# A decoder layer on eight cores: RMS norms as an epilogue on the products, layer norm sums beside the convolution, and the orders at both ends

## What is computed

```python
x = x + 0.5 * swiglu_ffn(rms_norm(x, ffn1_norm), ffn1_w_gu, ffn1_w_down)
# token_mixer on h = rms_norm(x, mix_norm); p = h @ w_in, split in 6 parts of 2048
u = gelu(ua);  v = layer_norm(gelu(va), ln_v_g, ln_v_b)
y_a = chunk_spatial_gating(u, v, w_s, b_s) @ w_pa     # causal, chunks of 128 tokens
g = glu_a * sigmoid(glu_b)
c = conv_31_taps_depthwise(g) + b_dw
c = silu(layer_norm(c, ln_c_g, ln_c_b));  y_b = c @ w_pb
x = x + (sigmoid(gate_a) * y_a + sigmoid(gate_b) * y_b) @ w_out
x = x + 0.5 * swiglu_ffn(rms_norm(x, ffn2_norm), ffn2_w_gu, ffn2_w_down)
y = rms_norm(x, final_norm)
```

## Time and profile before

| | |
|---|---|
| median of three runs | 3339.24 us |
| the profiled execution | 3340.61 us, span 3339.1 us on core 4 |
| spans of the eight cores | 3331.6 to 3339.1 us |
| TensorE (PE) busy | 3232.5 us, 97% of the span, 21555 matmuls |
| VectorE (DVE) busy | 856.8 us, 26%, 1448 instructions |
| ScalarE (ACT) busy | 467.0 us, 14%, 909 instructions |
| GpSimd (POOL) busy | 128.6 us, 4%, almost only DMA issues |
| mean granted TensorE clock, core 4 | 0.985 of 2.4 GHz |
| DMA | 284.30 MB moved, mean 85 GB/s |

### The profile page before, as it was taken

One profiled execution on the slowest core, in us unless ns is written; L12 is line 12 of the kernel. 1 busy time (PEld: TensorE's weight loads), 2 busy tenths in 40 slices (PEclk: granted clock), 3 DMA queues, 4 the chain that ended last, 5 costly groups with the idle time before them and its releaser, 6 DMA issues.

```text
span 3339.1 us, 51314 instructions; the slowest of 8 cores (3331.6 to 3339.1 us)
## 1 busy us (share of the span) xinstructions
PE 3232.5 (97%) x21555; PEld 2059.6 (62%) x21556; DVE 856.8 (26%) x1448; ACT 467.0 (14%) x909; POOL 128.6 (4%) x246
## 2 busy tenths in 40 slices
PE   5999999999999999898999999999999999999997
PEld 2566666666665576677666666666666666666664
DVE  2212113112114443326531111114212112112115
ACT  3100000000002121147210101002100000000002
POOL 0000000000000000000000000000000000000000
PEclk8999999999999999999999999999999999999998
DMA  6425624424427555522423333373334434334434
GB/s 162 73 54 104 108 54 81 75 54 88 76 54 174 110 120 118 118 59 51 106 53 76 76 76 68 64 187 68 64 60 86 76 57 84 69 63 84 76 53 125
DMA packets 74112, 284.30 MB, mean 85 GB/s; under 512 B 9888, under 2 KB 36768, under 8 KB 52000
## 3 DMA queue, kind: packets, MB, share of 16 engines
q0 software_dynamic: 34848, 216.62, 36.6%
q1 hardware_dynamic: 39040, 64.40, 6.8%
HBM read 468.14 MB, written 32.87 MB: 150 GB/s over the span
## 4 chain that ended last, share of the span: by engine, by line
PE 94%; DVE 2%; ACT 1%; DMA 1%; issue 1%; SPq 0%; DVEq 0%; ACTq 0%
PE ps L192 94%; ACT arena L195 1%; DVE arena L205 1%; DMA arena<-xin 1%; DVE arena L198 1%; ACT L195 0%; DVE arena L209 0%; DMA vsamp<-arena 0%; DMA arena<-gd 0%; DMA gd<-arena 0%; SPq L976 0%; DVEq L967 0%; DVE arena L201 0%; DVEq L953 0%; ACTq L967 0%
## 5 line engine op out<-in xcount | busy, mean ns | idle before, releaser
L192 PE MATMUL ps<-arena 128*128 128x364 bf16 (+5 forms) x21555 | 3232.5, 312 | 86.1 <-ACT arena L195 48.5
L192 PEld LDWEIGHTS ps<-arena 128*128 128x128 bf16 (+1 forms) x21556 | 2059.6, 98 | 1258.6 <-issue 129.7
L198 DVE TENSOR_TENSOR arena<-arena,ps 128x364 bf16<-128x364 f32 (+9 forms) x472 | 236.9, 514 | 1681.4 <-PE ps L192 1668.7
L195 ACT ACTIVATE arena<-ps 128x364 f32<-128x364 f32 (+1 forms) x528 | 242.0, 464 | 2404.6 <-PE ps L192 2359.3
L205 DVE SCALAR_TENSOR_TENSOR arena<-ps,arena 128x364 f32<-128x364 f32 (+5 forms) x451 | 241.1, 539 | 500.2 <-PE ps L192 499.9
L198 DVE TENSOR_TENSOR arena<-arena 128x512 bf16<-128x512 f32 (+7 forms) x168 | 185.3, 1115 | 67.1 <-PE ps L192 44.9
L195 ACT ACTIVATE arena<-arena 128x364 bf16<-128x364 f32 (+6 forms) x276 | 152.8, 631 | 270.0 <-PE ps L192 194.2
L205 DVE SCALAR_TENSOR_TENSOR arena<-arena 128x364 bf16<-128x364 f32 (+4 forms) x196 | 101.2, 593 | 1.8 <-DVE arena L209 0.2
L976 POOL DMA_DIRECT2D arena<-w_gu x88 | 46.8, 532 | 1178.0 <-PE ps L192 1112.9
L976 POOL DMA_DIRECT2D arena<-w_dn x64 | 33.9, 530 | 772.5 <-PE ps L192 772.5
L195 ACT ACTIVATE arena<-ps,arena 128x272 bf16<-128x272 f32 (+3 forms) x76 | 38.0, 500 | 113.3 <-PE ps L192 113.2
(11 more groups left out here) (10 smaller groups left out, 15.9 us busy)
## 6 DMA issues: line engine op xcount, KB each, us to landing
arena<-w_gu POOLq DMA_DIRECT2D x88, 1024.0 KB, 8.9
arena<-w_dn POOLq DMA_DIRECT2D x64, 704.0 KB, 7.1
arena<-w_glu POOLq DMA_DIRECT2D x16, 1024.0 KB, 10.3
arena<-w_gate POOLq DMA_DIRECT2D x16, 1024.0 KB, 9.4
arena<-w_pab POOLq DMA_DIRECT2D x16, 1024.0 KB, 9.7
arena<-w_v POOLq DMA_DIRECT2D x8, 1024.0 KB, 9.3
arena<-w_u POOLq DMA_DIRECT2D x8, 1024.0 KB, 8.1
arena<-w_out POOLq DMA_DIRECT2D x8, 1024.0 KB, 9.9
```

Source lines behind the costliest of these rows:

```text
L192: return P.op("pe", lambda e: e.matmul(out, lhsT, rhs, start=start, stop=stop), deps)
L195: return P.op("act", lambda e: e.activation(out=out, in_=in_, func=func, **kw), deps)
L198: return P.op("dve", lambda e: e.tensor_tensor(out=out, in0=in0, in1=in1, op=op), deps)
```

## The change

**Segments and columns.** The segments are 384, 384, 350 (then 320). In each chunk of 128 tokens the columns are stored by phase (token 4q + j at 32j + q), masks, spatial weights and halo are permuted alike on the host, and the last V tile has 64 rows instead of 94.

**The norms.** H is now x * g alone, written by ACT as each row is finished; rstd multiplies the products afterwards. DVE does that, so DVE now lets go of the banks of gate, GLU's b, U and the gates. For V, rstd goes through DRAM into a scale by partition (`RV`) of ACT's gelu.

```diff
+            def gate_part(bank, lg, s):
+                x0, n = segs[s]
+                gi_, bg = bank
+                ti, tmp, tfree = TMPS.get()
+                e = tt(tmp[:, 0:n], bg[:, 0:n], RSTD[:, x0:x0 + n], ALU.mult, deps=[lg, rstd[s]] + tfree)
+                banks.release(gi_, [e])
+                return ti, tmp, act(tmp[:, 0:n], tmp[:, 0:n], AF.Silu, deps=[e])
+
+            def up_part(bank, lu, jj, s, gp):
+                x0, n = segs[s]
+                ui_, bu = bank
+                ti, tmp, ea = gp
+                e = tt(tmp[:, 0:n], tmp[:, 0:n], RSTD[:, x0:x0 + n], ALU.mult, deps=[ea])
+                ed = tt(HID[:, jj, x0:x0 + n], tmp[:, 0:n], bu[:, 0:n], ALU.mult, deps=[e, lu, hid_free[s]])
+                banks.release(ui_, [ed])
+                TMPS.release(ti, [ed])
+                hid[s] = ed
```

```diff
+            def row(self, k, dep):
+                self.flush()
+                x0, n = self.x0, self.n
+                X = self.Xs[self.s][:, k, 0:n]
+                si, sq, sfree = self.ring.get()
+                self.pend.append((k, si, sq[:, 0:n], act(sq[:, 0:n], X, AF.Square, deps=[dep] + sfree)))
+                if self.Hout is not None:
+                    self.out[(self.s, k)] = act(self.Hout[:, k, x0:x0 + n], X, AF.Identity, deps=self.hdep + [ev_pv],
+                                                scale=pvc(self.gidx, k))
...
+                n = self.n
+                for (k, si, sq, ea) in self.pend:
+                    if k < self.direct:
+                        if self.ev is None:
+                            self.ev = ts(self.acc, sq, 1.0, 0.0, ALU.mult, ALU.add, deps=[ea])
+                        else:
+                            self.ev = tt(self.acc, self.acc, sq, ALU.add, deps=[ea, self.ev])
...
-            return [step(k) for k in range(KC)] + [finish]
+                        if self.bank is None:
+                            bi, bk, bfree = stat_banks.get()
+                            self.bank = (bi, bk)
+                            for q, (pi_, pt, e) in enumerate(self.parts):
+                                lm = mm(bk[:, 0:n], ONES, pt[:, 0:n], q == 0, False, deps=[e, e_ones] + bfree)
+                                if pi_ is not None:
+                                    self.ring.release(pi_, [lm])
+                        self.lm = mm(self.bank[1][:, 0:n], ONES, sq, False, k == KC - 1, deps=[ea])
+                        self.ring.release(si, [self.lm])
```

```diff
+            def units_by_row(tiles, s, tok):
+                x0, n = segs[s]
+                got = [(banks.get(), banks.get()) for _ in tiles]
+                last = {}
+                for k in range(KC):
+                    tok.prep(k)
+                    for (jj, slot, lev), ((_g, bg, gfree), (_u, bu, ufree)) in zip(tiles, got):
+                        W = wk(slot)
+                        lg = mm(bg[:, 0:n], W[:, k, 0:128], Hv[:, k, x0:x0 + n], k == 0, k == KC - 1,
+                                deps=[lev, hready[(s, k)]] + (gfree if k == 0 else []))
+                        last[jj] = (lg, mm(bu[:, 0:n], W[:, k, 128:256], Hv[:, k, x0:x0 + n], k == 0, k == KC - 1,
+                                           deps=(ufree if k == 0 else [])))
+                    tok.sum(k)
+                tok.finish()
+                for (jj, slot, lev), ((gi_, bg, _f), (ui_, bu, _h)) in zip(tiles, got):
+                    up_part((ui_, bu), last[jj][1], jj, s, gate_part((gi_, bg), last[jj][0], s))
```

**The convolution's layer norm.** A square on ACT of each conv output, four additions of 544 elements on DVE (`ln_sum`) per channel group, 16 matmuls of 272 in all behind that (`ln_phase`), `ln_apply` in phase order, and one contiguous silu of 1088 for each row. Five V tiles stand ahead of conv(15):

```diff
+        V_FIRST = 5
+        wi_v, slot_v, lev_v = wnext()
+        for (t, rows, hc) in vt[0:V_FIRST]:
+            v_tile(0, wk(slot_v), lev_v, t, rows, hc, x1_dead)
         conv(KC - 1)
...
+                got = []
+                for hi, lo, e in parts:
+                    b_, bk, bfree = stat_banks.get()
+                    mm(bk[:, 0:272], PHM[:, i, :], hi, True, False, deps=[e, e_ph] + bfree)
+                    got.append((b_, bk, mm(bk[:, 0:272], PHM[:, i, :], lo, False, True)))
...
-        side = [rowsum(q) for q in range(4)]
...
+        side = [nothing] * 2 + [ln_phase(i) for i in range(4)] + [nothing, ln_root]
+        side += [rowsum(q) for q in range(4)] + [nothing]
```

**V, U and the gates.** `v_out` sends both outputs after c = 2. U and the gates take rstd on DVE ahead of ACT:

```diff
-            u_ev[c] = act(U32[c % 2][:, x0:x0 + n], bk[:, 0:n], AF.Gelu_apprx_tanh, deps=[lm] + u_free[c % 2])
-            banks.release(bi, [u_ev[c]])
+            uo = U32[c % 2][:, x0:x0 + n]
+            e1 = tt(uo, bk[:, 0:n], RSTD[:, x0:x0 + n], ALU.mult, deps=[lm] + u_free[c % 2])
+            banks.release(bi, [e1])
+            u_ev[c] = act(uo, uo, AF.Gelu_apprx_tanh, deps=[e1])
...
+                ra = tt(sa[:, 0:n], bga[:, 0:n], R, ALU.mult, deps=[lga, us_all] + saf)
+                banks.release(gai, [ra])
+                rb = tt(sb[:, 0:n], bgb[:, 0:n], R, ALU.mult, deps=[lgb] + sbf)
+                banks.release(gbi, [rb])
+                ea = act(sa[:, 0:n], sa[:, 0:n], AF.Sigmoid, deps=[ra])
+                eb = act(sb[:, 0:n], sb[:, 0:n], AF.Sigmoid, deps=[rb])
```

```diff
+            def finish(self, on_pool=()):
+                self.flush()
+                er = root(self.bank, self.lm, self.x0, self.n)
+                self.rout[self.s] = er
+                if self.Hout is None:
+                    n, s = self.n, self.s
+                    for k in range(KC):
+                        X = self.Xs[s][:, k, 0:n]
+                        R = RSTD[:, self.x0:self.x0 + n]
+                        if k in on_pool:
+                            e = P.op("pool", lambda e, X=X, R=R: e.tensor_tensor(out=X, in0=X, in1=R, op=ALU.mult),
+                                     [er])
+                            self.out[(s, k)] = act(X, X, AF.Identity, deps=[e, ev_pv], scale=pvc(self.gidx, k))
+                        else:
+                            self.out[(s, k)] = stt(X, X, pvc(self.gidx, k), R, ALU.mult, ALU.mult, deps=[er, ev_pv])
```

551 lines of the change are left out of this document (311 added, 240 removed).

## The result

| | before | changed |
|---|---|---|
| median | 3339.67 us (4 runs) | 3302.12 us (4 runs) |
| ratio, with 95% interval | | 0.9889 (0.987 to 0.9909) |
| span of the slowest core | 3339.1 us (core 4) | 3299.1 us (core 6) |
| spans of the cores | 3331.6 to 3339.1 us | 3284.0 to 3299.1 us |
| DVE busy | 856.8 us, 26% | 1308.1 us, 40% |

The change is worth 1.1%, 37.6 us, and not the 91 that I had forecast; the time lies outside my range.

The account below looks back on a forecast made before the run. TensorE, busy 97%, was taken to bound the kernel. Terms -26, -12, +2, -11, -36, 0, -11, 0 and +3 sum to -91 us on 3339.1, so 3248 us, range 3222 to 3268.

Parts of the forecast that it names:

- What bounds the kernel: Whole kernel: TensorE busy 97%; gains only from fewer or narrower matmuls, places where it stands still, or lower-clock stretches.
- Start, -26: Before the first FFN: root and DVE's `stt` leave the path, prelude ends at 87.8 instead of 113.9 us.
- Norm ahead of GLU, -12: FFN1's following norm: 48 sums become 9, saving 6.2 us, and the 5.8 lost ahead of GLU go.
- GLU, +2: GLU and convolution: extra DVE work ahead of the first convolution costs 2 us, bounds 0 and 10.
- conv(15), -11: Last convolution: five V tiles ahead cover PE's 9.12 us idle but for 0.5, plus 2 lost by clock.
- V stage, -36: V product and layer norm: fewer sums, no waits for ACT, better clock, 42.4 us in all, less 6 lost.
- `w_out` and FFN2's way there, -11: `w_out` with its norm: 39 sums go, 6.0 us, and the 5.2 us lost there.
- The last norm, +3: From segment 0's last down product to the end: 55.3 us instead of 52.9, with GpSimd's multiply at 0.9.
- GpSimd and DVE hinder each other: Rival, last rows: the two take turns multiplying, adding 8.5 us, 3257; 3271 if GpSimd is near its upper bound; chance 0.16.
- DVE is late in letting go of banks: Rival, convolution and V stages: waits stay, now for DVE; V part -9 instead of -36, 3275 us; chance 0.12.
- FFN units waiting for DVE: Rival, slower than before: each FFN unit waits for DVE, 0.35 us a unit eating the gain; chance 0.03.
- my three signs of being wrong: FFN units show PE waiting for DVE, the start ends over 100, or DVE ends PE's V-stage waits.

Follow-up runs that it names:

- the kernel with four edits: Changed kernel with the old start transfer order, H of segments 1 and 2 issued earlier, a third GLU state-row buffer, last norm by DVE in portions: ratio 0.9753.
- the portions' own experiment: Changed kernel with the last norm finished by DVE alone, segments 0 and 1 three rows behind each following down product: 3279.87 us in a single run.
- the experiment: Changed kernel without the five V tiles ahead of the last convolution, which follow it as before: 3314.80 us in a single run.

## Why the prediction was wrong, point by point

The step that failed is one and the same in three terms of the sum: at a border between two stages TensorE was let go on as soon as its data and banks seemed to be there, and what stands ahead on DVE's queue, with what that waits for, was put at nothing or too low. The terms are the start (-26, measured -7), norm and GLU (-10, +1) and the last norm (+3, +16): 43 of the 51 us missing, though some 5 us at the start and 6 at the norm ahead of GLU have other causes, as told below.

- *What bounds the kernel:* right. The FFN pays nothing for rstd on DVE, the sums' matmuls are gone (121 fewer with 60 small ones added, as the sum's 182 less has it), and the change gives back half of its gain by order. That the kernel with four edits comes to 3257 us, near the forecast, is in part luck: its last norm is not the forecast one, and takes 45.8 us by the portions' own experiment where the sum had 55.3.
- *Start, -26; it was -7.* Two terms failed. x0's end was put at 36 and came at 41.2; undoing the transfers' order alone gives 12.8 us. x1, whose landing at 57 my path went through, was in by 51.1 and held up nothing. And the sum lacked a term: I had PE go on from segment to segment with what was in the banks, and never asked what stands ahead of H on DVE. That is 4.2 and 5.0 us of waiting; order alone takes half of it back, 8.3 us with the clock behind it (6 by the times). I had asked what is queued ahead for POOL and SP, and not for DVE.
- *Norm ahead of GLU, -12, and GLU, +2; together +1.* The 6.2 us of sums went, as all sums did, but the 5.8 us lost there were put down to the norm because the trace named ACT. With the norm gone PE lost time there still, now waiting 3.39 us for a weight tile, and putting the writes of x off only moved the loss. The +2 for DVE's queue had an upper bound of 10, and PE's wait was 8.4 us on the slowest core (3.5 and 2.2 before): six banks cover 15 us of products only if DVE starts on time, and it started with a 9.8 us wait for an output. Taking that wait away took half of PE's.
- *conv(15), -11:* right; -13 by the table and 13 by the experiment.
- *V stage, -36; -32.* Mechanism and size right. The waits for ACT are gone, the clock is 0.97 (I had said 1.00); the reciprocal ahead of the row sums costs 3.95 us in the trace, part of the 6 that I had set aside.
- *`w_out` and FFN2's way there, -11; -5.* The norm's wait is gone. A wait of 2.96 us for ACT at 3220.15 has come, behind the block in which DVE splits three segments' sums ahead of segment 0's last products. The rest, about 3 us, was not followed up and stays open.
- *The last norm, +3; +16.* The estimate of GpSimd's row was good: 0.9 for 384 columns, and 0.82 measured for 320 alone. But the sum used it for eight rows beside DVE, and there a pair takes 1.27. Its two blocks and the last rows were to last 7.2, 7.2 and 5.6 us and lasted 10.2, 10.2 and 8.3: 8.7 us of the 13, so the rival "GpSimd and DVE hinder each other" came true at its price of 8.5. The other 5 are smaller pieces that the sum lacked, among them a table load of 1.28 us ahead of the first root and products at the lower clock behind each wait. The mechanism was wrong too, by luck at no cost in the number: I had ACT's queue hold the squares, and it was DVE's, in which finished rows of one segment stand ahead of the residual sums of the next. The block itself, which I had put into the sum as if it had to be there, is what the portions win back. The Trainium skill, "GPSIMD Engine Reference", section Elementwise — side-by-side cycle accounting, would give 0.70 us for 320 columns as an estimate; the trace has 0.82, and that decides. The Trainium skill, "SBUF — State Buffer", section Terms, has the loser wait for the whole operation: by that the pair would be the sum of both, 9.3 us in segment 2; side by side it was 8.28, near it but not the same, and the measurement decides.
- *The rivals:* "DVE is late in letting go of banks" came true at one place, the first convolution, and hardly in the V stage, where I had expected it: DVE ends PE's waits there, but they are 1.05, 0.92 and 3.95 us. FFN units waiting for DVE: not seen. Of my three signs of being wrong two came: the start ended over 100 (106.9), and DVE is what ends PE's waits in the V stage.
- *The chances:* 0.87 for faster by over 2% left 0.13 for what happened. The parts' errors were not independent of one another: in four of them (start, first convolution, end of FFN2, last norm) an order on DVE that I had not written down had a share.

## What to carry to other kernels

When work moves to an engine that was three quarters idle, its busy share says nothing of the risk; write out its queue at each border between stages and ask which instruction stands ahead of the one that the busiest engine needs, and what that one waits for. A block of finished results (a norm's last rows) belongs in portions between the steps that feed the next sums. Of loads at the start, issue at once what is needed first, and behind a wait whatever is not; and a wait named in the trace may hide another right behind it (of PE's 8.4 us at the first convolution half stood behind the wait for `cst`), so price its removal by what ends next.

## What the runs showed of the hardware

GpSimd's multiplication of 320 fp32 columns takes 0.82 us alone and 1.06 beside DVE, whose own goes from 0.47 to an estimated 1.1 (8.28 us less six by 0.47, over five); for 384 columns the pair takes 1.27 a row. Sharing rows between these two engines saved 1.0 us of 9.3 against one behind the other, and lost 0.8 against DVE alone doing all sixteen (7.49). A weight tile that lands in 9.5 us by the median of the changed kernel took 26.9 in the start (median of four, issued by 3.3 us), where twelve x groups are issued by 35.2; the first eight x groups took 19.7. A contiguous silu of 1088 columns takes 1.28 us, a strided one of 1024 2.67.
